# A hybrid attention and state-space layer on one core: order of the first loads, place of the modulation weights, and the first dense chunk computed in halves

## The reference, cut to what matters

```
mod = silu(cond) @ w_ada + b_ada            # cond: one vector for context, one for latent; w_ada 1024 x 6144
sh1, sc1, g1, sh2, sc2, g2 = split(mod, 6)
h = rmsnorm(x, g_pre_mix) * (1 + sc1) + sh1
y = token_mixer(h)       # h @ w_in (1024 x 10304), attention, state-space scan, projections
x = x + g1 * rmsnorm(y, g_post_mix)
h = rmsnorm(x, g_pre_ffn) * (1 + sc2) + sh2
y = expert_choice_ffn(h) # 16 experts, gate/up 1024 x 2048 and down 2048 x 1024 each
x = x + g2 * rmsnorm(y, g_post_ffn)
```

## Time and profile before

| | us |
|---|---|
| median of 3 runs | 1711.43 (1710.7 to 1713.13) |
| span of the profiled execution (first to last instruction) | 1708.6 |
| PE busy | 1529.9 (90%) |
| DVE busy | 473.3 (28%) |
| ACT busy | 337.0 (20%) |
| POOL busy | 90.0 (5%) |
| TensorE's mean granted clock, as a share of full | 0.978 |

### The profile page before, as it was taken

One profiled execution on the slowest core, in us unless ns is written; L12 is line 12 of the kernel. 1 busy time (PEld: TensorE's weight loads), 2 busy tenths in 40 slices (PEclk: granted clock), 3 DMA queues, 4 the chain that ended last, 5 costly groups with the idle time before them and its releaser, 6 DMA issues.

```text
span 1708.6 us, 15782 instructions
## 1 busy us (share of the span) xinstructions
PE 1529.9 (90%) x6391; PEld 711.7 (42%) x6391; DVE 473.3 (28%) x1111; ACT 337.0 (20%) x873; POOL 90.0 (5%) x121
## 2 busy tenths in 40 slices
PE   6999999999999999999998897877888877978787
PEld 2655555565545555556433332222222222322233
DVE  3437878740015555433111110000010000101002
ACT  2336565510023332012000000000000000010101
POOL 0003222200000001000000000000000000000000
PEclk9999999999999999999999999999999999999999
DMA  8234343324321535548999999999999999999995
GB/s 358 99 113 173 124 168 129 105 81 187 133 97 64 214 132 199 219 195 370 405 430 431 433 431 430 432 431 432 433 429 430 431 430 434 431 432 430 431 429 248
DMA packets 29608, 512.42 MB, mean 300 GB/s; under 512 B 3505, under 2 KB 3889, under 8 KB 9825
## 3 DMA queue, kind: packets, MB, share of 16 engines
q1 hardware_dynamic: 23472, 490.67, 68.7%
q0 software_dynamic: 5920, 20.61, 3.6%
q10 hardware_dynamic: 144, 0.13, 0.0%
HBM read 506.59 MB, written 4.82 MB: 299 GB/s over the span
## 4 chain that ended last, share of the span: by engine, by line
PE 52%; DMA 34%; DVE 9%; ACT 3%; issue 2%; SPq 0%; DVEq 0%; ACTq 0%
DMA arena<-in_expert_chunks 33%; PE psum L1051 14%; PE psum L703 7%; PE psum L461 6%; PE psum L675 5%; PE psum L472 3%; PE psum L1022 2%; PE psum L750 2%; PE psum L852 2%; DMA arena<-in_mixer_chunks 1%; ACT arena L1504 1%; DVE arena L1920 1%; PE psum L1071 1%; PE psum L742 1%; PE psum L484 1%
## 5 line engine op out<-in xcount | busy, mean ns | idle before, releaser
L1051 PE MATMUL psum<-arena 128*64 128x512 f32 x1856 | 435.0, 624 | 85.5 <-DMA arena<-in_expert_chunks 85.5
L1051 PEld LDWEIGHTS psum<-arena 128*64 128x64 f32 x1856 | 139.8, 143 | 366.7 <-issue 293.9
L1071 PE MATMUL psum<-arena 128*64 128x512 f32 x896 | 203.5, 608 | 48.4 <-DMA arena<-in_expert_chunks 48.4
L461 PE MATMUL psum<-arena 128*128 128x384 f32 x512 | 169.0, 487 | 0.0
L2315 DVE TENSOR_TENSOR arena<-arena,psum 128x512 f32<-128x512 f32 x30 | 20.6, 688 | 434.1 <-PE psum L1051 412.2
L1071 PEld LDWEIGHTS psum<-arena 128*64 128x64 f32 x896 | 63.8, 139 | 180.3 <-issue 116.1
L703 PE MATMUL psum<-arena 128*128 128x384 f32 x384 | 127.9, 486 | 0.0
L472 PE MATMUL psum<-arena 128*128 128x512 f32 x288 | 126.3, 594 | 0.0
L461 PEld LDWEIGHTS psum<-arena 128*128 128x128 f32 x512 | 96.2, 190 | 65.9 <-issue 3.4
L1657 ACT ACTIVATE arena<-psum 32x512 f32<-32x512 f32 (+1 forms) x70 | 38.2, 546 | 422.7 <-PE psum L1071 391.0
L1677 ACT ACTIVATE arena<-psum 128x512 f32<-128x512 f32 x30 | 17.9, 597 | 395.6 <-PE psum L1051 370.1
(11 more groups left out here) (282 smaller groups left out, 1277.2 us busy)
## 6 DMA issues: line engine op xcount, KB each, us to landing
arena<-in_expert_chunks SPq DMA_DIRECT2D x82, 4096.0 KB, 22.0
arena<-in_mixer_chunks SPq DMA_DIRECT2D x40, 2048.0 KB, 7.9
arena<-in_expert_chunks SPq DMA_DIRECT2D x24, 2048.0 KB, 13.1
arena<-cs_rows POOLq DMA_DIRECT2D x24, 512.0 KB, 5.0
arena<-in_expert_chunks SPq DMA_DIRECT2D x6, 1024.0 KB, 18.3
arena<-in_h_cm POOLq DMA_DIRECT2D x8, 256.0 KB, 3.0
out_state<-arena POOLq DMA_DIRECT2D x8, 256.0 KB, 2.6
arena<-in_x_cm SPq DMA_DIRECT2D x1, 1536.0 KB, 6.7
```

What stands on the lines that cost most here:

```text
L461: mm = pe.matmul(b[:, 0:NTOK], w[:, k, ct * P:(ct + 1) * P], src[:, k, :], start=k == 0, stop=k == KT - 1)
L1051: mm = pe.matmul(psum[HALF * q:HALF * (q + 1), hidden_banks(e, u)[up], :], x_in[:, k, :], w[q][:, k, :], start=k == 0, stop=k == KT - 1, t ...
L1071: mm = pe.matmul(psum[HALF * q:HALF * (q + 1), 5 + e % 2, :], hT[:, KT * u + k, :], w[q][:, k, :], start=bool(not u and k == 0), stop=bool ...
```

## The change

x is loaded ahead of the vectors. The four modulation pieces go to buffers "a", "b", "d", "e", with "d" at 153 KiB and "e" at 170 KiB, so that no load waits before ("x", 0). Chunk ("x", 4) comes in two transfers of four blocks each: the first is issued between the second and the third modulation piece (semaphore w_in_slot0), the second after the fourth (w_in_rest). SP's order is then x, vectors, pieces 0 and 1, first half of ("x", 4), pieces 2 and 3, second half, ("x", 5), lam, dt columns, constants, with no wait between them.

TensorE runs 18 matmuls of the identity with 256 constant columns into PSUM bank 7 as soon as the constants are there. It computes the first four tiles in halves (`first_tile`), four banks held open: two first halves, piece 2, one first half, the transposes of piece 2, piece 3, one first half, the transposes of piece 3, and then the four second halves. ACT squares blocks 0 to 3 of x and DVE blocks 4 to 7. DVE scales blocks 0 to 3 of x after the broadcast, and blocks 4 to 7 after it has written h for the first half.

```diff
-    todo = [(("ada", n), "w_ada", ADA_ORDER[n] * CW, 0, slot) for n, slot in enumerate((0, 1, "a", "b"))]
+    todo = [(("ada", n), "w_ada", ADA_ORDER[n] * CW, 0, slot) for n, slot in enumerate("abde")]
...
-                       "c": early_6}
+                       "c": early_6, "d": at(153, KT, CW), "e": at(170, KT, CW)}
...
             pe.wait_ge(sem("const_in"), 16)
+            for _ in range(18):
+                pe.matmul(psum[:, 7, 0:2 * P], ident, cst[:, 0:2 * P], start=True, stop=True)
             pe.wait_ge(sem("x_sum_ready"), 1)
...
-            for j in range(1, 4):
-                first_ada(j)
-                ada_cm(j - 1)
+            first_ada(1)
+            ada_cm(0)
+            ada_cm(1)
+            first_n = n_p[0] + 2
+            def first_tile(ct, half):
+                w = weight_slot[0]
+                if not half:
+                    pe.wait_ge(sem("p_free"), first_n + ct - 3)
+                for k in range(4 * half, 4 * half + 4):
+                    if not ct:
+                        pe.wait_ge(sem("h1_dve"), k + 1)
+                    if not ct and half:
+                        pe.wait_ge(sem("h1_act"), k - 3)
+                    mm = pe.matmul(psum[:, (first_n + ct) % 4, 0:NTOK], w[:, k, ct * P:(ct + 1) * P], h1T[:, k, :],
+                                   start=k == 0, stop=k == KT - 1)
+                return mm
+            pe.wait_ge(sem("w_in_slot0"), 16)
+            first_tile(0, 0)
+            first_tile(1, 0)
+            first_ada(2)
+            first_tile(2, 0)
+            ada_cm(2)
+            first_ada(3)
+            first_tile(3, 0)
+            pe.wait_ge(sem("x_normed"), 1)
             ada_cm(3)
-
-            for j in (4, 5):
-                for ct in range(4):
-                    cm_tile(("x", j), ct, by_block=j == 4 and not ct)
+            pe.wait_ge(sem("w_in_rest"), 16)
+            n_p[0] += 4
+            for ct in range(4):
+                p_done(first_tile(ct, 1))
+            chunk_used(("x", 4))
+            for ct in range(4):
+                cm_tile(("x", 5), ct)
...
+            sp.dma_start(x_cm.rearrange("p k n -> p (k n)"), t_in["x_cm"]).then_inc(sem("x_in"), 16)
             sp.dma_start(vecs, t_in["vectors"]).then_inc(sem("vec_in"), 16)
-            sp.dma_start(x_cm.rearrange("p k n -> p (k n)"), t_in["x_cm"]).then_inc(sem("x_in"), 16)
...
+                if n == chunk_no["ada", 2]:
+                    load_first(0, "w_in_slot0")
+                if n == chunk_no["x", 4]:
+                    load_first(1, "w_in_rest")
+                    continue
...
-            act.activation(x_sq..., x_cm..., ACT.Square)
+            act.activation(x_sq[:, 0:4]..., x_cm[:, 0:4]..., ACT.Square)
...
+            act.wait_ge(sem("x_normed"), 1)
             act.wait_ge(sem("aff1_ready"), 2)
...
+            dve.wait_ge(sem("x_in"), 16)
+            link(dve.tensor_tensor(x_sq[:, 4:8], x_cm[:, 4:8], x_cm[:, 4:8], ALU.mult))
             dve.wait_ge(sem("x_sq_ready"), 1)
...
-            b = x_take()
-            x_free(dve.tensor_tensor(x_cm, x_cm, b[:, 0:NTOK].unsqueeze(1).broadcast_to([P, KT, NTOK]), ALU.mult))
+            by_rstd = x_take()[:, 0:NTOK].unsqueeze(1).broadcast_to([P, 4, NTOK])
+            x_free(dve.tensor_tensor(x_cm[:, 0:4], x_cm[:, 0:4], by_rstd, ALU.mult))
...
             for half in range(2):
+                if half:
+                    dve.tensor_tensor(x_cm[:, 4:8], x_cm[:, 4:8], by_rstd, ALU.mult).then_inc(sem("x_normed"), 1)
                 ada_cm(2 * half)
                 ada_cm(2 * half + 1)
                 affine(aff1, 8, 0, 48, 4 * half, 4).then_inc(sem("aff1_ready"), 1)
                 dve.wait_ge(sem("aff1_ready"), half + 1)
+                if half:
+                    dve.wait_ge(sem("x_normed"), 1)
```

More of the change, by code:

```diff
@@ L449, in chunk_used, with cm_tile @@
                 AT["chunk_end"][chunk_no[key]] = (signal, n_p[0] if value is None else value)
-            def cm_tile(key, ct, src=None, by_block=False):
-                src = h1T if src is None else src
+            def cm_tile(key, ct):
                 w = chunk(*key)
@@ L456, in cm_tile @@
                 for k in range(KT):
[L457 to L461, removed]
+                    mm = pe.matmul(b[:, 0:NTOK], w[:, k, ct * P:(ct + 1) * P], h1T[:, k, :],
                                    start=k == 0, stop=k == KT - 1)
@@ L1176, in used, with load_first @@
                 sp.wait_ge(sem(name), value)
+            def load_first(half, name):
+                sp.dma_start(slots[0][:, 4 * half:4 * half + 4].rearrange("p k n -> p (k n)"),
+                             mixer_w[chunk_no["x", 4], :, 4 * half * CW:4 * (half + 1) * CW]).then_inc(sem(name), 16)
             for n in range(NM - 1):
                 slot, m = chunk_slot[n], last_in_slot[n]
+                if n == chunk_no["ada", 2]:
[3 more added lines that the diff above has]
+                    continue
                 if slot in (2, 3) and m is None:
@@ L1185, in _ @@
                 sp.dma_start(weight_slot[slot].rearrange("p k n -> p (k n)"), mixer_w[n]).then_inc(sem(f"w_in_slot{slot}"), 16)
-                if n == chunk_no["x", 4]:
+                if n == chunk_no["x", 5]:
                     sp.dma_start(lam_in.rearrange("p a d -> p (a d)"), t_in["lam"]).then_inc(sem("lam_in"), 16)
-                if n == chunk_no["x", 5]:
                     sp.dma_start(dt_w.rearrange("p k n -> p (k n)"), dt_cols).then_inc(sem("dtw_in"), 16)
@@ L1397, in _ @@
             act.wait_ge(sem("x_in"), 16)
-            act.activation(x_sq.rearrange("p k n -> p (k n)"), x_cm.rearrange("p k n -> p (k n)"), ACT.Square)\
+            act.activation(x_sq[:, 0:4].rearrange("p k n -> p (k n)"), x_cm[:, 0:4].rearrange("p k n -> p (k n)"), ACT.Square)\
                .then_inc(sem("x_sq_ready"), 1)
```

## The result

The changed kernel takes 1713.99 us (median of 13 runs, 1711.99 to 1717.91); the kernel before, in 13 runs, 1711.43 (1709.66 to 1713.29). The ratio is 1.0020 with a 95% interval of 1.0013 to 1.0027: slower by 2.6 us in the medians, at the bound of what can be told. The forecast was 1709.9 with a range to 1713.4; the time lies above the range and moved the other way. The profiled execution took 1713.69 us over a span of 1711.9, 3.3 us above the span of before. Five of the 13 runs took 1716.35 to 1717.91 us and the other eight 1711.99 to 1714.08; the profile is of one of the eight, and no profile shows what the five did more.

What follows compares the result with a forecast made beforehand. Transfers were taken to bound the front, with holes in PE. Half tile start 23.05 plus 28.5 ends ("x", 4) at 51.6, not 53.1; span 1708.6 - 1.5 = 1707.1, plus 2.8 gives 1709.9 us, range 1707.3 to 1713.4.

Steps and rivals of the forecast that it cites:

- the start of the identity matmuls: TensorE's start: the 18 matmuls begin when the constants land, at 4.2 us, bounds 3.84 and 7.4.
- 7.74 + c/2: Length of the 36 identity records; c, the low-clock time, taken as 5 us, so they end at 14.4 (13.7 to 15.2).
- rival (2): TensorE's start: identity matmuls end late, clock staying low, and delay x_sum's matmuls; 1715 the middle case, chance 0.11.
- What bounds the kernel: Transfers bound the front, PE having holes; what the front gains or loses reaches the end at about its own size.
- x first takes back what the halved square wins: Front, before x_sum: halving wins 1.4 us, later vectors take back 1.2; x_sum ready at 13.8 instead of 14.03.
- Landings of the later transfers: Front's loads: pieces 2 and 3 land at 25.0 and 29.9, the second half of ("x", 4) at 32.4, costing nothing.
- All pieces at full clock: TensorE's front: each of the four modulation pieces takes 1.9 us; piece 0 took 3.64 before.
- The first half tile, given the start: TensorE's first dense matmuls: start at 23.05 after PE idles 1.5 us; 22.4 to 23.8 by the bounds.
- The exposed waits: Half tiles on PE: two waits of 0.75 us for banks ACT empties, one of 1.3 us for h.
- rival (1): Before the first half tile: the clock falls in the idle 1.5 us, losing 1.75 us of matmuls; 1711.7, chance 0.18.
- Rival (3): Front: bank waits and h's wait shrink (2.8 us in all), clock never falls; up to 4 us, 1707.4, chance 0.09.
- Rival (4): After the front: a wait in the scan or expert-weight stream takes up the gain; 1711.4, chance 0.07.

Runs made afterwards that it cites:

- reordered: The changed kernel with the vectors loaded before x and TensorE's front reordered to cover three waits; 1707.86 us, ratio 0.9981 to the kernel before.
- vec_first: The changed kernel with the vectors loaded ahead of x again; 1710.07 us, ratio 0.9999 to the kernel before.
- x_quarters: The changed kernel with x still first but loaded in four transfers, 3 KB rows; 1710.41 us, ratio 0.9998 to the kernel before.
- no_warm: The changed kernel, x still first, without the 18 identity matmuls; 1712.85 us, ratio 1.0010 to the kernel before.
- warm8: The changed kernel, x still first, with 8 identity matmuls instead of 18; 1711.30 us, ratio 0.9999 to the kernel before.
- reordered14: The kernel of reordered with 14 identity matmuls instead of 18; 1707.98 us, ratio 0.9980 to the kernel before.
- old_warm: The kernel before with only the 18 identity matmuls added; 1713.21 us, ratio 1.0009 to the kernel before.
- filled14: The kernel of reordered14 with three more identity matmuls in the gap before the first half tile; 1707.31 us, ratio 0.9979 to the kernel before.
- old_x_first: The kernel before with only x loaded ahead of the vectors; 1711.11 us, ratio 1.0001 to the kernel before.

## Why the prediction was wrong

The step that failed is the start of the identity matmuls: "with x beside them instead of the vectors I take 4.2 (bounds 3.84 and 7.4, when x has landed too; the row is nearest)". It was 7.91, past the far bound: the constants landed just behind x, whose transfer took 6.9 us. The row that I called nearest was of the constants beside the vectors, with rows of 1.4 KB; what I had to place was the constants beside rows of 12 KB. The Trainium skill's rule on turns was cited, yet not carried through to the row sizes, which the transfers' sizes give; with it and these rows the landing comes close to x's.

From there my own terms give the result. The end of the identity matmuls was put at start + 7.74 + c/2; with 7.91 and the measured 18.63, c, the time at half clock, is 5.96 us, inside my 3.5 to 6.5. They ended 4.2 us later than forecast, the issue came 4.5 later (56.39 against 51.9), and the direction with it: 1709.9 and the 4.2 us give 1714.1, measured 1713.99. This is rival (2), with a late start in the place of a clock that stays low; I gave it 0.11 and priced a start at 7.4 as 1713.1, inside it.

Point by point:

- What bounds the kernel, and that the front's shift arrives at the end at its own size: right for these two profiles, 3.0 us at the issue, 3.3 in the span. Over all profiles the two later stretches scatter by up to 2.7 and 2.3 us (last section), so a single span can't show a shift of this size for sure.
- x first takes back what the halved square wins: right, the vectors landed at 8.3 (forecast 7.9), x_sum at 14.1 instead of 13.8. With the vectors first it came at 12.9, and the 18 matmuls hid that.
- Landings of the later transfers: put too early. In the changed kernel the second half of ("x", 4) landed at 4.55 + 29.7 = 34.3 (forecast 32.4), and SP's issues were through at 12.8 instead of 6; TensorE came later than all of it, so it cost nothing. In reordered piece 3's landing at 31.36 (forecast 29.9) did set the end of the front. Why they are later is open.
- All pieces at full clock: right, 1.92 us each.
- The first half tile, given the start: right; vec_first began it at 23.13 (forecast 23.05) after 1.64 us idle (1.5).
- The exposed waits: right, 0.72, 0.72 and 1.52 us against 0.75, 0.75 and 1.3. The stretch from the half tile to the end of ("x", 4) took 29.0 us in vec_first (28.5), so the change with the vectors first wins 1.0 us in the front, not the 1.5 of the sum.
- The clock in the idle time before the first half tile, rival (1): not in the changed kernel's profile, vec_first's, x_quarters', no_warm's or reordered's, but in warm8's and reordered14's, at the same 1.64 us. It costs the forecast 1.7 us in the half tiles, of which reordered14 loses only 0.4 at the issue. That the changed kernel's profile was spared is luck, not something the prediction had a reason for.
- Rival (3), the covers: right in kind, in another kernel. Covering the three waits (3.0 us) won 2.4 us, with piece 3's landing as the new bound.
- Rival (4), a loss later: no sign of it.

## What to carry to other kernels

A transfer on a second queue was not independent of the first here: the landings fit engines shared row by row, so the small one with 1 KB rows landed at 7.86 us beside 12 KB rows and at 4.54 beside 3 KB rows. Before the order of two loads is changed, list every transfer in flight beside them on other queues, and what waits for each. Work that is only there to raise an engine's clock must not be able to stand in front of real work: give it an input that is surely early, and size it by its latest start.

## What the runs showed of the hardware

- The clock's fall after a gap is not fixed by its length here: after 1.64 to 1.66 us idle it was at half in the next 3.5 us in warm8, reordered14 and old_warm, and full in five others, no_warm among them. It fell after 1.27 us idle in filled14 and not after 3.78 us in old_warm.
- Nor is the time to full clock fixed: the 36 identity records took from 9.68 us (reordered) to 10.82 (old_warm), which is an estimate of 3.9 to 6.2 us at half clock by the prediction's 7.74 + c/2.
- The same in the mixer: the stretch from the issue of ("x", 0) to the first expert load took 646.3 to 646.7 us in ten of the twelve profiles, 647.8 in no_warm, and 645.1 in old_x_first, whose clock stayed at 1.00 after the wait near 104 us where the kernel before had 0.69.
- From the first expert load to the end it took 1008.4 to 1008.8 us in six profiles (before, changed, vec_first, no_warm, reordered, filled14), 1009.4 in old_warm and 1010.0 to 1010.7 in the other five. This amount is not explained.
